# Attention units pass the engines one step further apart: scores two units ahead, exponentials of the next unit between the copies of the transposed one

## What is computed

```python
logits = einsum('bqhd,bshd->bhqs', q, k) * scale + bias     # causal mask inside the bias
p = softmax(logits)                                           # with sinks: exp(sink) joins the sum
y = einsum('bhqs,bshd->bqhd', p, v)
# three-branch layer: y = g0 * y_compressed + g1 * y_selected + g2 * y_window
```

## Time and profile before

| what | value |
|---|---|
| median of 3 runs | 1134.16 us (1131.32 to 1137.84) |
| the profiled execution's own time | 1134.58 us |
| its span in the profile | 1131.6 us |
| TensorE busy | 1063.2 us (94%) |
| VectorE busy | 693.1 us (61%) |
| ScalarE busy | 563.4 us (50%) |
| granted TensorE clock, mean over the span | 0.971 |
| gate stage, first scores to last output | 143.8 to about 203 us |
| sink stage | 481.3 to about 517.6 us |
| branch stage | 802 to about 904.3 us |

### The profile page before, as it was taken

One profiled execution on the slowest core, in us unless ns is written; L12 is line 12 of the kernel. 1 busy time (PEld: TensorE's weight loads), 2 busy tenths in 40 slices (PEclk: granted clock), 3 DMA queues, 4 the chain that ended last, 5 costly groups with the idle time before them and its releaser, 6 DMA issues.

```text
span 1131.6 us, 23550 instructions
## 1 busy us (share of the span) xinstructions
PE 1063.2 (94%) x8892; PEld 1034.1 (91%) x8892; DVE 693.1 (61%) x1334; ACT 563.4 (50%) x1083; POOL 206.5 (18%) x221
## 2 busy tenths in 40 slices
PE   5888988999999998999999999999799999999998
PEld 5778888999999997989999999999788899999997
DVE  5478664777775446755666674477445366666643
ACT  3354456456664334675544453357456554444431
POOL 5000000053341212004211113300000051111230
PEclk9888999999999999999999999999789899999999
DMA  9433332455556556504566657664500055665740
GB/s 278 84 96 93 115 111 76 135 165 174 181 181 208 185 186 149 177 11 112 149 184 181 179 167 202 209 159 141 184 1 2 1 150 160 180 182 161 215 143 38
DMA packets 225602, 161.38 MB, mean 143 GB/s; under 512 B 7379, under 2 KB 222776, under 8 KB 225530
## 3 DMA queue, kind: packets, MB, share of 16 engines
q1 hardware_dynamic: 222592, 154.23, 45.3%
q0 software_dynamic: 2544, 6.04, 3.2%
q10 hardware_dynamic: 394, 0.13, 0.1%
HBM read 158.28 MB, written 2.10 MB: 142 GB/s over the span
## 4 chain that ended last, share of the span: by engine, by line
PE 81%; DVE 8%; ACT 5%; issue 2%; DMA 2%; POOL 1%; SPq 0%; DVEq 0%; ACTq 0%; POOLq 0%
PE bank L585 22%; PE bank L587 22%; PE bank L586 22%; PE bank L836 4%; PE bank L824 2%; PE bank L581 2%; PE bank L808 2%; PE bank L809 2%; DVE w_lo L1474 1%; ACT work L1256 1%; DMA raw<-w_in_in 1%; DVE big L1531 1%; ACT w_hi L1082 1%; ACT big L1270 1%; PE bank L736 1%
## 5 line engine op out<-in xcount | busy, mean ns | idle before, releaser
L1474 DVE TENSOR_TENSOR w_lo<-raw,w_hi 128x1024 fp32r<-128x1024 f32 (+2 forms) x281 | 356.8, 1273 | 222.0 <-ACT w_hi L1082 220.1
L585 PE MATMUL bank<-hh,w_hi 128*128 128x256 f32 x1384 | 398.0, 288 | 16.1 <-ACT work L1227 8.1
L586 PE MATMUL bank<-hl,w_hi 128*128 128x256 f32 x1384 | 394.9, 285 | 0.0
L587 PE MATMUL bank<-hh,w_lo 128*128 128x256 f32 x1384 | 394.7, 285 | 0.0
L1082 ACT ACTIVATE w_hi<-raw 128x1024 fp32r<-128x1024 f32 (+2 forms) x281 | 299.0, 1081 | 169.7 <-PE bank L587 159.8
L585 PEld LDWEIGHTS bank<-hh,w_hi 128*128 128x128 f32 x1384 | 267.7, 193 | 20.7 <-issue 12.7
L586 PEld LDWEIGHTS bank<-hl,w_hi 128*128 128x128 f32 x1384 | 267.8, 194 | 0.1
L587 PEld LDWEIGHTS bank<-hh,w_lo 128*128 128x128 f32 x1384 | 267.8, 193 | 0.0
L585 PE MATMUL bank<-hidh,w_hi 128*128 128x256 f32 x672 | 188.7, 281 | 1.2 <-POOL hidl L2134 1.1
L586 PE MATMUL bank<-hidl,w_hi 128*128 128x256 f32 x672 | 188.2, 280 | 0.0
L587 PE MATMUL bank<-hidh,w_lo 128*128 128x256 f32 x672 | 188.2, 280 | 0.0
(11 more groups left out here) (257 smaller groups left out, 1334.0 us busy)
## 6 DMA issues: line engine op xcount, KB each, us to landing
raw<-ffn_w_gu_in SPq DMA_DIRECT2D x88, 512.0 KB, 5.0
raw<-w_ff_in SPq DMA_DIRECT2D x64, 512.0 KB, 4.2
raw<-w_in_in SPq DMA_DIRECT2D x26, 512.0 KB, 6.2
raw<-ffn_w_down_in SPq DMA_DIRECT2D x32, 384.0 KB, 4.1
raw<-ffn_w_down_in SPq DMA_DIRECT2D x32, 320.0 KB, 3.4
raw<-b_w_in_in SPq DMA_DIRECT2D x14, 512.0 KB, 4.7
raw<-a_w_qkv_in SPq DMA_DIRECT2D x10, 512.0 KB, 4.5
raw<-w_out_in SPq DMA_DIRECT2D x8, 512.0 KB, 4.5
```

What stands on the lines that cost most here:

```text
L585: pe.matmul(o, ah, bh, start=start, stop=False)
L586: pe.matmul(o, ah, bl, start=False, stop=False)
L587: return pe.matmul(o, al, bh, start=False, stop=stop)
L1474: dve.tensor_tensor(tile_view(w_lo, n), raw_view(n), tile_view(w_hi, n).bitcast(F32), ALU.subtract)\
```

## The change

It reorders the three queues in all three runs of units, and alters what is put between them:

- PE: the scores of the first two units go ahead of the loop, then `keep_busy(12)` once; inside, transposes(u), then scores(u+2), rows_to_columns(u-1), values(u). The `keep_busy(4)` of every unit of the sink and branch stages is gone (the one after the last unit stays). In the gate stage one gate tile comes before transposes(u) and one behind it.
- ACT: the exponentials of u+1 are spread over the copies of u: copy 0, exponentials 0, copy 1, exponentials 1, copy 2, exponentials 2, copy 3, (output copy), exponentials 3. In the gate stage: exponentials 0, gate, copies 0 and 1, exponentials 1, copies 2 and 3, exponentials 2, gate, output copy, exponentials 3.
- DVE: soften runs two units ahead; it now waits for the transposes of u-2 group by group. The second half of `gelu` moves behind the soften of unit 9.
- The compressed keys and values are made at unit 8, behind its transposes, instead of at unit 9.
- Three small arrays (minimum, sum, sink sum) get three slots instead of two. `s_buf` keeps two.

```diff
--- before.py
+++ after.py
@@ -231,12 +231,12 @@
-        mn = sb("mn", [P, 2, HU])
-        ssum = sb("ssum", [P, 2, HU])
+        mn = sb("mn", [P, 3, HU])
+        ssum = sb("ssum", [P, 3, HU])
         rinv = sb("rinv", [P, HU])
         sinks = sb("sinks", [P, 16])
         nsinks = sb("nsinks", [P, 16])
-        esink = sb("esink", [P, 2, HU])
+        esink = sb("esink", [P, 3, HU])
@@ -851,18 +851,19 @@
                                       src[:, 2 * c:2 * c + 2, :].rearrange("p a b -> p (a b)"), ident[:, :])
                 close_bank(mm, f"Y{u}", Y_BANK)
 
-            def units(first, last, between=None, before=None):
+            def units(first, last, early=None, middle=None):
+
                 scores(first)
+                scores(first + 1)
+                keep_busy(12, T_BANK)
                 for u in range(first, last + 1):
-                    if before:
-                        before(u)
-                    if u < last:
-                        scores(u + 1)
-                    if between:
-                        between(u)
-                    else:
-                        keep_busy(4, T_BANK)
+                    if early:
+                        early(u)
                     transposes(u)
+                    if middle:
+                        middle(u)
+                    if u + 2 <= last:
+                        scores(u + 2)
                     if u > first and u - 1 in Y_UNITS:
                         rows_to_columns(u - 1)
                     values(u)
@@ -872,11 +873,7 @@
             pe.wait_ge(*ev["qT3"])
             pe.wait_ge(*ev["kT3"])
 
-            def two_gates(u):
-                gate_tile(8 + 2 * u)
-                gate_tile(9 + 2 * u)
-
-            units(0, 3, two_gates)
+            units(0, 3, lambda u: gate_tile(8 + 2 * u), lambda u: gate_tile(9 + 2 * u))
 
 
             pe.wait_ge(y_done, 4)
@@ -1017,7 +1014,7 @@
 
                     def compressed(u):
 
-                        if u != 9:
+                        if u != 8:
                             return
                         pe.wait_ge(cg, 1)
                         pe.wait_ge(late_in, 16 * N_LATE)
@@ -1034,7 +1031,7 @@
                         close_bank(mm, "cv", T_BANK + 1)
                         pe.wait_ge(*ev["ck"])
                         pe.wait_ge(*ev["cv"])
-                    units(8, 19, before=compressed)
+                    units(8, 19, middle=compressed)
 
                 square_projection(f"wo{layer}", yh, yl, lambda k: (y_done, (8 if layer == 0 else 12) - (2 if k < 4 else 0)))
                 main_variance(f"ffn2_{layer}")
@@ -1253,8 +1250,8 @@
                 for j in range(2):
                     h = PAIRS[k] + 2 * j
                     s = s_buf[u % 2][:, h, 0:U["nk"]]
-                    ins = act.activation(s, s, ACT.Exp, scale=-1.0, bias=mn[:, u % 2, h:h + 1],
-                                         accum_out=ssum[:, u % 2, h:h + 1])
+                    ins = act.activation(s, s, ACT.Exp, scale=-1.0, bias=mn[:, u % 3, h:h + 1],
+                                         accum_out=ssum[:, u % 3, h:h + 1])
                     if j == 0:
                         step(ins)
                     else:
@@ -1269,24 +1266,51 @@
                 h = PAIRS[k]
                 act.activation(PT[0:o.shape[0], h:h + 3:2, 0:o.shape[2], :], o, ACT.Copy).then_inc(pt_ready, 1)
 
-            def unit(u, gates_of=None, also=None):
+            def sink_exp(u):
+                i = u - FIRST_UNIT["swa"] + 1
+                act.wait_ge(es_in, i)
+                act.activation(esink[:, u % 3, :], esink[:, u % 3, :], ACT.Exp).then_inc(es_out, 1)
+
+            def units(first, last, early=None, middle=None, ahead=None):
+
+                def next_exps(u, *groups):
+                    for k in groups:
+                        if u < last:
+                            exps(u + 1, k)
+
                 for k in range(4):
-                    exps(u, k)
-                if also:
-                    also()
-                if "sink" in UNITS[u]:
-                    i = u - FIRST_UNIT["swa"] + 1
-                    act.wait_ge(es_in, i)
-                    act.activation(esink[:, u % 2, :], esink[:, u % 2, :], ACT.Exp).then_inc(es_out, 1)
-                if gates_of is not None:
-                    for j in gates_of:
-                        gate(j)
-                for k in range(4):
-                    take_transposed(u, k)
-                if u - 1 in Y_UNITS and u not in FIRST_UNIT.values():
-                    take_columns(u - 1)
-                if u in LAST_UNIT.values():
-                    take_columns(u)
+                    exps(first, k)
+                if "sink" in UNITS[first]:
+                    sink_exp(first)
+                if ahead:
+                    ahead()
+                for u in range(first, last + 1):
+                    if early:
+                        next_exps(u, 0)
+                        early(u)
+                        take_transposed(u, 0)
+                        take_transposed(u, 1)
+                        next_exps(u, 1)
+                        take_transposed(u, 2)
+                        take_transposed(u, 3)
+                        next_exps(u, 2)
+                        middle(u)
+                    else:
+                        take_transposed(u, 0)
+                        next_exps(u, 0)
+                        take_transposed(u, 1)
+                        next_exps(u, 1)
+                        take_transposed(u, 2)
+                        next_exps(u, 2)
+                        take_transposed(u, 3)
+                        if middle:
+                            middle(u)
+                    if u - 1 in Y_UNITS and u > first:
+                        take_columns(u - 1)
+                    next_exps(u, 3)
+                    if u < last and "sink" in UNITS[u + 1]:
+                        sink_exp(u + 1)
+                take_columns(last)
 
             def take_columns(u):
 
@@ -1295,8 +1319,7 @@
                 act.activation(yh[:, U["y"]:U["y"] + 4, P * U["t"]:P * U["t"] + P],
                                psum[Y_BANK][:, :].rearrange("p (c q) -> p c q", c=4), ACT.Copy).then_inc(y_hi, 1)
 
-            for u in range(4):
-                unit(u, (8 + 2 * u, 9 + 2 * u))
+            units(0, 3, lambda u: gate(8 + 2 * u), lambda u: gate(9 + 2 * u))
             prefetch(ST["branch"] + 3)
             for fc in range(KC):
                 prefetch(ST["branch"] + fc + 4)
@@ -1392,8 +1415,7 @@
                     tile(n + 9)
                     act.activation(vT[:, 0, :], psum[1][:, 0:T], ACT.Copy).then_inc(ev_act, 1)
                     prefetch(n + 12)
-                    for u in range(4, 8):
-                        unit(u)
+                    units(4, 7)
                 else:
                     for kv in range(2):
                         tile(n + 8 + kv)
@@ -1432,15 +1454,16 @@
                         act.wait_ge(cg_in, 1)
                         act.activation(c_tmp[:, 1, :], c_tmp[:, 0, :], ACT.Exp, scale=-2.0 * math.sqrt(2.0 / math.pi)).then_inc(cg_e, 1)
 
-                    def compressed_keys():
+                    def compressed_keys(u):
+                        if u != 8:
+                            return
                         act.wait_ge(*filled["ck"])
                         for i in range(2):
                             ins = act.activation(ckh[HD * i:HD * i + HD, :, :], psum[T_BANK][0:HD, 0:2 * NC]
                                                  .rearrange("p (g c) -> p g c", g=2), ACT.Copy)
                         ins.then_inc(q_hi, 1)
 
-                    for u in range(8, 20):
-                        unit(u, also={8: gelu_exp, 9: compressed_keys}.get(u))
+                    units(8, 19, middle=compressed_keys, ahead=gelu_exp)
                 prefetch(ST[f"wo{layer}"] + 3)
                 late_norm(f"ffn2_{layer}")
                 name = f"gu{layer}"
@@ -1751,33 +1774,33 @@
 
                 U = UNITS[u]
                 nk = U["nk"]
-                if u >= 2:
-                    dve.wait_ge(*filled[f"T{u - 2}3"])
                 for k in range(4):
+                    if u >= 2:
+                        dve.wait_ge(*filled[f"T{u - 2}{k}"])
                     dve.wait_ge(*filled[f"S{u}{k}"])
                     for j in range(2):
                         h = PAIRS[k] + 2 * j
                         h8 = 8 * U["sink"] + h if "sink" in U else None
                         ins = dve.tensor_tensor_reduce(out=s_buf[u % 2][:, h, 0:nk], in0=s_out(u, k)[:, j, :], in1=U["bias"](h),
                                                        scale=-U["scale"], scalar=-LOW1 if h8 is None else nsinks[:, h8:h8 + 1],
-                                                       op0=ALU.add, op1=ALU.min, accum_out=mn[:, u % 2, h:h + 1])
+                                                       op0=ALU.add, op1=ALU.min, accum_out=mn[:, u % 3, h:h + 1])
```

(25 more changed lines are left out.)

## The result

The changed kernel takes 1159.84 us (median of 4 runs, 1157.57 to 1162.19), the kernel before 1132.93 us in the same comparison: ratio 1.023, 95% interval 1.019 to 1.027. The profiled execution took 1157.57 us with a span of 1155.5 us. The prediction was 1155 us, range 1132 to 1172. Against the kernel before that is 27 us more, where 20 were forecast.

The account below looks back on a forecast made before the run. TensorE's string of instructions plus its gaps was taken to bound each stage; 1134.6 us + 2 (gate) + 0.5 (sink) + 1.2 (branch at today's clock) + 16.7 (clock) = 1155 us, range 1132 to 1172.

Parts of the forecast that it names:

- The gap: Transposes, sink and branch stages: group 3 waits for copy 1 behind a pair of exponentials, +2.7 and +8.55 us.
- The clock term: Branch stage: clock falls around units 10, 13 and 16, putting 170 instructions at 0.5, +16.7 us (bounds 0 and 50).
- the time at 0.5 in the branch stage: Sign to check: granted clock at 0.5 for some 30 to 40 us of the branch stage, against about 27 before.
- Fill and compressed keys: Branch stage: fill net -9.5 us, longer wait for compressed keys at unit 8 +1.3, work shifted to low clock +0.9.
- The block: 24 fill instructions added once per stage: 2.8 us at full clock, 5.1 in the branch stage.
- The one wait of 3.0 us at the scores of unit 10: Branch stage: compressed keys' banks come free only with copies 2 and 3, a 3.0 us wait, +1.3.
- Gate stage: +2 us: tile waits covered -4.4, fill +2.8, two bank waits +0.7 each, y_low wait +1.9, tanh misfits.
- Sink stage: +0.5 us: fill -0.9, later copy 1 +2.7, shorter stall of unit 7 -1.3.
- The stall of unit 7: Sink stage: TensorE's 1.73 us wait for exponentials loses its 1.3 us above the usual 0.4.
- (a): Rival, whole kernel: the clock behaves as today, 1138.3 us; chance 0.27.
- (b): Rival, transposes: pair between copies 0 and 1 not waited for and clock holds, 1124 to 1127 us; chance 0.14.
- (c): Rival, branch stage: once low, clock stays low until the output projection, some 1170 to 1185 us; chance 0.12.

Follow-up runs that it names:

- e3: The changed kernel with ScalarE's copies 0 and 1 back to back, ahead of the next unit's exponentials, in the sink and branch stages; 1134.7 us.
- e2: The changed kernel with four fill matmuls put back ahead of the transposes of each sink and branch unit but the first; 1167.6 us.
- e1: The kernel before, all orders kept, without the four fill matmuls of each unit of the sink and branch stages; 1132.1 us.
- e6: As e3, and in the gate stage without the block of 24 fill instructions and with y_low(u-1) ahead of soften(u+2); 1136.1 us.
- e7: As e6, with the fill block ahead of the sink and branch stages cut from 24 to 8 instructions; 1130.3 us.
- e9: As e7, but in unit 8 ScalarE makes all four copies and the compressed keys' copy before the exponentials of unit 9; 1129.4 us.
- e10: As e9, with eight fill instructions added behind the values of units 10, 13 and 16 only; 1128.9 us.

## Why the prediction was right, and where not

**The size and the sign** were right: 1155 against 1159.8. The step that decided was to read ScalarE's queue as it stands, copy 0, pair, copy 1, and to ask who is queued behind group 3 on TensorE; e3 shows that this one place carries most of the loss. That the sum came so close is partly luck: it was 2.3 us too high in the branch stage and 1.0 in the sink stage, 1.6 too low in the gate stage, and it had nothing for the 5.2 us outside the stages.

**The gap** was taken as 8.55 us in the branch stage and 2.7 in the sink stage. Its size was right. From start to start group 3 comes 8.1 and 2.7 us later than in e3; the brackets of the timeline show less (5 and 2.3). At low clock TensorE's own instructions cover a part: 0.18 to 0.37 us in brackets in units 9, 14 and 15, none in 12 and 18. Too large was what it costs in the sink stage: 1.6 us, because two other waits had been hidden behind it.

**The clock term**, +16.7 us, fits in size: 47 to 49 us more low time, at 0.31 to 0.39 us each, are 15 to 19, and the branch stages of the changed kernel and e3 give some 14. The working behind it does not fit as well: 215 instructions ran in the three long stretches instead of 170, and each cost less than the 0.107 us that it used. Its reasoning was half right. The prediction made the missing fill the main cause and the gap a remark. The runs turn that around. Fill back and gap kept (e2): 98 us of low time. Gap removed and fill left out (e3): 71, as before. But without either in the old order (e1) it is 101, and with the branch stage of e3 6 us earlier (e6) it is 90. So the missing fill has an effect too, and where a stage lies in time seems to have one; how the low time divides between them and the gap isn't settled. Where the clock falls and how long it stays low was right for the changed kernel itself: it fell behind units 10, 13 and 16, as said, and stayed for 13 to 17 us.

**A slip in its own check:** the time at 0.5 in the branch stage was forecast at 30 to 40 us, against 27 before. Counted in the same way it was 68 (75 and 31 with the stretch at the end of the stage), and should have been forecast near 60: 170 instructions at 0.213 us are 36 us on top of 27.

**Fill and compressed keys.** No run measures these terms one by one. The prediction has -9.5 + 1.3 + 0.9 = -7.3 us for the branch stage without the pair and at today's clock; in e3, which has no pair and 3.5 us more at 0.5 there, the stage is 5.5 us shorter than before. The block took 3.4 us and not 5.1, because the clock rose soon after its start (814.75). The one wait of 3.0 us at the scores of unit 10 did not come: there are three short ones of 0.63, 0.56 and 0.45 us, in sum as long as the 1.7 us before, so +1.3 was too much. In the gate stage the block took 2.84 us (2.8).

**Gate stage:** +2 forecast, +3.6 measured. The wait for y_low was there (1.67 us against 1.9), so were the two waits for tanh (0.66 each against 0.7). Not foreseen: just behind the 1.67 us the clock fell for 3.4 us, and the gate tile there took 4.6 us instead of 3.1. This fall is in the profiles of all six kernels that have the wait, and in none of the four where y_low comes first and the block is gone (e6, e7, e9, e10), nor in the two with the old order.

**Sink stage:** +0.5 forecast, -0.5 measured. The stall of unit 7 fell from 1.73 to 0.60 us as forecast. Two things make up the 1 us and more: before, the clock was at 0.5 for 3.4 us at the start of this stage, after, nowhere in it; and the gap cost 1.6 us and not 2.7.

**Outside the stages** nothing was forecast, and 5.2 us came. The low stretch over the end of the branch stage is 6.8 us long instead of 3.4, about 1 us. Most of the rest has one form. Between the gate and the sink stage every kernel with the changed gate stage takes 282.0 us, and both with the old one 279.8 and 280.0 (before, e1), at clock 1.0 in both. There 24 projection matmuls, one weight tile, take 2.88 us instead of 2.85; between the sink and the branch stage it is 2.87 against 2.86, and behind the branch stage 2.88 against 2.85. Over 89, 92 and 73 tiles that is 2.5, 1.2 and 1.9 us. All ten kernels in the new order have it. What links it to the order of the attention units was not tried and stays open.

**The rivals.** (a), the clock as before, falls: 120 us of low time. With it falls the reading of the Trainium skill's page "TensorE: Matmul & The Clock Gate", section "What's actually happening", by which idleness closes the gate, in so far as e1's 20 us at 0.5 had TensorE busy for 19.6 of them; that the gap matters at all (e3), and the falls behind the 1.67 us in the gate stage, speak for it. (b), the pair not waited for, falls by the 0.87 us in the timeline. Nor is its time, 1124 to 1127 us, that of the kernel without the pair: e3 takes 1134.7, with 5 us of it in the slower tiles outside the stages. (c), never back up, falls: it rose at 860, 888 and 915.

## What to carry to other kernels

In a string of work that one engine bounds, read the other engines' queues for what stands between two steps that this engine needs one after the other; a half idle engine can still put 1 us into each unit. Spread an engine's free work behind its urgent work, not between. And where the clock already falls now and then, a gap can cost more than its length: here gaps of 11 us from start to start cost 18 to 25. Compare versions by time and by time at low clock, over ten runs rather than three, because a change in one stage can move the clock in the next.

## What the runs showed of the hardware

One us at clock 0.5 costs this kernel 0.2 to 0.45 us by the spread of the runs of one and the same kernel, 0.34 by the branch stages of the changed kernel and e3, and 0.48 by those of e1 and the kernel before. The spread of the runs (1129 to 1145 us in e1) goes with the clock. Filling the gaps with useless matmuls lowered the time at 0.5 from 120 to 80 and 57 us at unchanged order. And a stage can lose what an earlier one gained: e6 saved 6.1 us in the gate stage and got 19 us more low time behind it. The same stretch of projection matmuls at clock 1.0 ran at 2.85 us a tile in two kernels and at 2.88 in all the others.
